# Near scores of a chunked gated linear attention: one product per tile for the diagonal and the levels of 2, 4 and 8

## What is computed

```
b = jnp.cumsum(gi, axis=-2)
o_inter = jnp.einsum('bhtk,bhkv->bhtv', qi * jnp.exp(b), state)
diff = b[:, :, :, None, :] - b[:, :, None, :, :]
decay = jnp.exp(jnp.where(causal, diff, -jnp.inf))
scores = jnp.einsum('bhtk,bhsk,bhtsk->bhts', qi, ki, decay)
o = o_inter + jnp.einsum('bhts,bhsv->bhtv', scores, vi)
```

## Time and profile before

| what | value |
|---|---|
| median of 3 runs | 1216.65 us (1216.47 to 1219.16) |
| the profiled execution | 1214.66 us |
| its span | 1212.5 us |
| TensorE busy | 1183.7 us, 98% of the span |
| VectorE busy | 796.3 us, 66% |
| ScalarE busy | 510.9 us, 42% |
| GpSimd busy | 110.5 us, 9% |

### The profile page before, as it was taken

The page is one execution under the profiler, slowest core; times in us unless marked ns, Lnnn a source line. Parts: engine busy times, 40 slices in busy tenths (PEclk is TensorE's granted clock), DMA queues, the critical chain, the costliest instruction groups (busy, mean ns, idle before and its releaser), DMA issues.

```text
span 1212.5 us, 18972 instructions
## 1 busy us (share of the span) xinstructions
PE 1183.7 (98%) x7577; PEld 1055.5 (87%) x7577; DVE 796.3 (66%) x1071; ACT 510.9 (42%) x646; POOL 110.5 (9%) x166
## 2 busy tenths in 40 slices
PE   6999999999999999999999999999999999999997
PEld 5789999998889987868887788888889999998887
DVE  5788888766786567676563256665878888762232
ACT  6445544561213645455343322233535554552322
POOL 2000000002220123333020001100000000000000
PEclk9999999999999999999999999999999999999999
DMA  9423333337983121212211445633123333322211
GB/s 367 153 73 112 110 108 109 113 99 268 329 293 124 37 69 37 66 39 71 70 62 44 139 157 181 215 108 104 36 73 117 109 109 109 107 96 96 96 61 71
DMA packets 115130, 143.55 MB, mean 118 GB/s; under 512 B 4085, under 2 KB 102785, under 8 KB 115073
## 3 DMA queue, kind: packets, MB, share of 16 engines
q1 hardware_dynamic: 106800, 113.32, 28.2%
q0 software_dynamic: 8064, 29.36, 6.9%
q10 hardware_dynamic: 208, 0.08, 0.0%
HBM read 140.65 MB, written 2.10 MB: 118 GB/s over the span
## 4 chain that ended last, share of the span: by engine, by line
PE 87%; DVE 7%; ACT 4%; issue 1%; POOL 1%; DVEq 0%; ACTq 0%; POOLq 0%
PE PS L794 28%; PE PS L550 16%; PE PS L552 15%; PE PS L551 15%; PE PS L873 4%; PE PS L913 1%; PE PS L595 1%; PE PS L597 1%; PE PS L596 1%; PE PS L708 1%; DVE ACC L1725 1%; ACT WH L1107 1%; PE PS L900 1%; PE PS L883 1%; DVE ACC0b L1736 1%
## 5 line engine op out<-in xcount | busy, mean ns | idle before, releaser
L1623 DVE TENSOR_TENSOR WL<-RAW,WH 128x2048 fp32r<-128x2048 f32 (+2 forms) x55 | 120.6, 2194 | 131.8 <-ACT WH L1107 131.7
L550 PE MATMUL PS<-HH,WH 128*128 128x512 f32 (+2 forms) x488 | 186.4, 382 | 4.3 <-DVE HL L1651 2.9
L1107 ACT ACTIVATE WH<-RAW 128x2048 fp32r<-128x2048 f32 (+2 forms) x55 | 100.6, 1829 | 199.5 <-PE PS L552 193.0
L552 PE MATMUL PS<-HH,WL 128*128 128x512 f32 (+2 forms) x488 | 178.9, 367 | 0.0
L551 PE MATMUL PS<-HL,WH 128*128 128x512 f32 (+2 forms) x488 | 178.8, 366 | 0.0
L794 PE MATMUL PS<-HH,WH 128*128 128x256 f32 x576 | 162.5, 282 | 0.4 <-DVE WL L1910 0.4
L794 PE MATMUL PS<-HL,WH 128*128 128x256 f32 x576 | 162.1, 281 | 0.0
L794 PE MATMUL PS<-HH,WL 128*128 128x256 f32 x576 | 162.1, 281 | 0.0
L550 PE MATMUL PS<-UH,WH 128*128 128x512 f32 (+1 forms) x416 | 148.2, 356 | 0.0
L552 PE MATMUL PS<-UH,WL 128*128 128x512 f32 (+1 forms) x416 | 147.3, 354 | 0.0
L551 PE MATMUL PS<-UL,WH 128*128 128x512 f32 (+1 forms) x416 | 147.2, 354 | 0.0
(11 more groups left out here) (304 smaller groups left out, 2308.4 us busy)
## 6 DMA issues: line engine op xcount, KB each, us to landing
RAW<-in_ffn_w_in_dram SPq DMA_DIRECT2D x42, 1024.0 KB, 5.1
ADAW<-in_w_ada_dram POOLq DMA_DIRECT2D x56, 512.0 KB, 5.4
RAW<-in_w_in_mix_dram SPq DMA_DIRECT2D x22, 1024.0 KB, 5.2
RAW<-in_ffn_w_down_dram SPq DMA_DIRECT2D x16, 1024.0 KB, 5.0
ADA<-in_w_ada_dram SPq DMA_DIRECT2D x16, 512.0 KB, 10.0
RAW<-in_ffn_w_down_dram SPq DMA_DIRECT2D x7, 768.0 KB, 4.3
RAW<-in_w_out_dram SPq DMA_DIRECT2D x3, 1024.0 KB, 5.0
XST<-in_x_dram SPq DMA_DIRECT2D x4, 512.0 KB, 5.1
```

The lines of the kernel that those rows point to most:

```text
L550: mm(ps, whi, ahi, start=start, stop=False)
L552: return mm(ps, wlo, ahi, start=False, stop=stop)
L1107: A(WH[slot(n)][:, 0:size], RAW[slot(n)][:, 0:size], ACT.Copy).then_inc(unit_hi, 1)
L1623: V.tensor_tensor(WL[s][:, 0:size], RAW[s][:, 0:size], WH[s][:, 0:size].bitcast(F32), ALU.subtract)\
```

## The change

The levels of 64, 32, 16 and 8 stay as masks, but only the first three keep a plane of `KP` and of `QP` each. The fourth plane of `KP` now holds every key, all 512 columns, scaled once: its reference is the second token of its quad (four tokens). `QQ` holds for each tile 192 columns: the 128 queries of the tile, scaled against the reference of their own quad, and then 64 queries, the later four tokens of each block of eight, scaled against the reference of the quad before theirs. One product of the fourth plane with these 192 columns gives both the scores within a quad (diagonal and the levels of 2 and 4) and the level of 8. `score_diagonal` is gone. Near0 keeps its eight products; near1 and near2 now each treat two tiles, with one product of 64 and one of 192 columns a tile, and both wait for all near products (`prep` 11 of 15). Near1 uses bank 5 and near2 bank 4; the far product of 256 columns moves from bank 4 to bank 5. A factor within a quad can now exceed one, since the reference token can stand ahead of its key or behind its query; therefore the log decay of a token is held at or above -50 ln 2 (`DECAY_FLOOR`, `LN_FLOOR`).

```diff
-    LN_FLOOR = 2.0 ** -63
+    LN_FLOOR = 2.0 ** -50
+    DECAY_FLOOR = -50 * 0.6931471805599453
...
-        KP = place("KP", [P, 6, T], 69632)
-        QP = place("QP", [P, 6, T // 2], 92160)
+        QP = place("QP", [P, 3, T // 2], 92160)
+        QQ = place("QQ", [P, TT, P + 64], 95232)
...
-        LEVELS = [64, 32, 16, 8, 4, 2]
+        LEVELS = [64, 32, 16, 8]
+        QUAD = 4
+
+        PREP = 15
+
+        def quads(ap):
+
+            return ap.rearrange("p (n b) -> p n b", b=QUAD)
...
                 cc = PREPS[p]["c"]
                 pool.wait_ge(cum, p + 1)
                 if p:
-                    pool.wait_ge(score_done, 6 * before_prep(p) + 3)
-                for l, B in enumerate(LEVELS):
+                    pool.wait_ge(score_done, 5 * before_prep(p) + 3)
+                for l, B in enumerate(LEVELS[0:3]):
                     h = B // 2
                     cb = blocks(cc, B)
                     mid = cb[:, :, h - 1:h].to_broadcast([P, T // B, h])
                     nc.gpsimd.tensor_tensor(QP[:, l, :].rearrange("p (n h) -> p n h", h=h), cb[:, :, h:B], mid,
                                             ALU.subtract).then_inc(diffs, 1)
-                for l, B in enumerate(LEVELS):
+                for l, B in enumerate(LEVELS[0:3]):
                     h = B // 2
                     cb = blocks(cc, B)
                     mid = cb[:, :, h - 1:h].to_broadcast([P, T // B, h])
                     nc.gpsimd.tensor_tensor(blocks(KP[:, l, :], B)[:, :, 0:h], mid, cb[:, :, 0:h],
                                             ALU.subtract).then_inc(diffs, 1)
+                cq = quads(cc)
+                nc.gpsimd.tensor_tensor(quads(KP[:, 3, :]), cq[:, :, 1:2].to_broadcast([P, T // QUAD, QUAD]), cq,
+                                        ALU.subtract).then_inc(diffs, 1)
+                ct = cc.rearrange("p (t n b) -> p t n b", n=P // 8, b=8)
+                nc.gpsimd.tensor_tensor(QQ[:, :, P:P + 64].rearrange("p t (n b) -> p t n b", b=4), ct[:, :, :, 4:8],
+                                        ct[:, :, :, 1:2].to_broadcast([P, TT, P // 8, 4]), ALU.subtract).then_inc(diffs, 1)
...
                 p, r = prep_of(a), rows_of(a)
                 bank = 4 + g % 2
-                pe.wait_ge(prep, 18 * p + 2 + 4 * (g + 1))
+                pe.wait_ge(prep, PREP * p + (6 if g == 0 else 11))
                 if g == 0 and a:
+                    pe.wait_ge(evac_v, a)
+                if g == 1 and a:
                     pe.wait_ge(evac_a, 2 * a)
-                if g == 1 and a:
-                    pe.wait_ge(evac_v, a)
                 if g == 2:
-                    pe.wait_ge(near_done, 6 * a + 2)
+                    pe.wait_ge(near_done, 7 * a + 2)
                 for j in range(2):
-                    l = 2 * g + j
-                    for t in range(TT):
-                        ins = mm(PS[:, bank, 256 * j + 64 * t:256 * j + 64 * t + 64],
-                                 KP[r, l, t * P:(t + 1) * P], QP[r, l, 64 * t:64 * t + 64], start=True, stop=True)
-                ins.then_inc(score_done, 1)
-
-            def score_diagonal(a):
-                p, r = prep_of(a), rows_of(a)
-                q, k = PREPS[p]["q"], PREPS[p]["k"]
-                pe.wait_ge(near_done, 6 * a + 4)
-                for t in range(TT):
+                    if g == 0:
+                        for t in range(TT):
+                            ins = mm(PS[:, bank, 256 * j + 64 * t:256 * j + 64 * t + 64],
+                                     KP[r, j, t * P:(t + 1) * P], QP[r, j, 64 * t:64 * t + 64], start=True, stop=True)
+                        continue
+                    t = 2 * g - 2 + j
                     tok = slice(t * P, (t + 1) * P)
-                    ins = mm(PS[:, 5, tok], k[r, tok], q[r, tok], start=True, stop=True)
+                    mm(PS[:, bank, 64 * j:64 * (j + 1)], KP[r, 2, tok], QP[r, 2, 64 * t:64 * (t + 1)], start=True, stop=True)
+                    ins = mm(PS[:, bank, 128 + 192 * j:128 + 192 * (j + 1)], KP[r, 3, tok], QQ[r, t, :], start=True, stop=True)
                 ins.then_inc(score_done, 1)
 
             def score_far(a):
                 p, r = prep_of(a), rows_of(a)
-                pe.wait_ge(prep, 18 * p + 18)
+                pe.wait_ge(prep, PREP * p + PREP)
                 if a:
                 ins.then_inc(score_done, 1)
-                pe.wait_ge(near_done, 6 * a + 6)
+                pe.wait_ge(near_done, 7 * a + 5)
                 for j in range(2):
-                    ins = mm(PS[:, 4, 256 * j:256 * (j + 1)], W512[r, j * P:(j + 1) * P], W512[r, 256:512],
+                    ins = mm(PS[:, 5, 256 * j:256 * (j + 1)], W512[r, j * P:(j + 1) * P], W512[r, 256:512],
                              start=True, stop=True)
                 ins.then_inc(score_done, 1)
...
                         score_levels(a, 2)
-                        score_diagonal(a)
...
             def near_factors(p):
                 exp_ln_tables()
-                act.wait_ge(diffs, 12 * p + 6)
+                act.wait_ge(diffs, 8 * p + 3)
                 A(QP[:, :, :], QP[:, :, :], ACT.Exp).then_inc(exps, 1)
-                for l, B in enumerate(LEVELS):
-                    act.wait_ge(diffs, 12 * p + 7 + l)
+                for l, B in enumerate(LEVELS[0:3]):
+                    act.wait_ge(diffs, 8 * p + 4 + l)
                     kk = blocks(KP[:, l, :], B)[:, :, 0:B // 2]
                     A(kk, kk, ACT.Exp).then_inc(exps, 1)
+                act.wait_ge(diffs, 8 * p + 7)
+                A(QQ[:, :, 0:P], KP[:, 3, :].rearrange("p (t c) -> p t c", c=P), ACT.Exp, scale=-1.0).then_inc(exps, 1)
+                act.wait_ge(diffs, 8 * p + 8)
+                A(QQ[:, :, P:P + 64], QQ[:, :, P:P + 64], ACT.Exp).then_inc(exps, 1)
+                act.wait_ge(exps, 10 * p + 8)
+                A(KP[:, 3, :], KP[:, 3, :], ACT.Exp).then_inc(exps, 1)
 
             def copy_far(a):
 
-                act.wait_ge(score_done, 6 * a + 5)
+                act.wait_ge(score_done, 5 * a + 4)
                 act.wait_ge(evac_v, a + 1)
                 diag = SC[:, :].rearrange("p (i x) -> p i x", x=5 * P)
                 A(diag[0:64, :, 64:P], PS[0:64, 6, 0:256].rearrange("p (i x) -> p i x", x=64), ACT.Copy)
                 A(SC[:, :].rearrange("p (i x) -> p i x", x=2 * T + 2 * P)[:, :, P:2 * P],
                   PS[:, 6, 256:512].rearrange("p (i x) -> p i x", x=P), ACT.Copy).then_inc(evac_a, 1)
-                act.wait_ge(score_done, 6 * a + 6)
+                act.wait_ge(score_done, 5 * a + 5)
                 A(SC[:, 0:2 * T].rearrange("p (i x) -> p i x", x=T)[:, :, T // 2:T],
-                  PS[:, 4, :].rearrange("p (i x) -> p i x", x=T // 2), ACT.Copy).then_inc(evac_a, 1)
+                  PS[:, 5, :].rearrange("p (i x) -> p i x", x=T // 2), ACT.Copy).then_inc(evac_a, 1)
...
                 dve.wait_ge(exps, 10 * p + 2)
                 V.tensor_tensor(QU[:, :], QU[:, :], q, ALU.mult).then_inc(prep, 1)
                 V.tensor_tensor(KL[:, :], KL[:, :], k, ALU.mult).then_inc(prep, 1)
-                for l, B in enumerate(LEVELS):
+                for l, B in enumerate(LEVELS[0:3]):
                     h = B // 2
                     dve.wait_ge(exps, 10 * p + 4)
                     qp = QP[:, l, :].rearrange("p (n h) -> p n h", h=h)
@@ -2095,8 +2121,16 @@
                     dve.wait_ge(exps, 10 * p + 5 + l)
                     kp = blocks(KP[:, l, :], B)[:, :, 0:h]
                     V.tensor_tensor(kp, kp, blocks(k, B)[:, :, 0:h], ALU.mult).then_inc(prep, 1)
+                dve.wait_ge(exps, 10 * p + 8)
+                V.tensor_tensor(QQ[:, :, 0:P], QQ[:, :, 0:P], q.rearrange("p (t c) -> p t c", c=P), ALU.mult).then_inc(prep, 1)
+                dve.wait_ge(exps, 10 * p + 9)
+                near = QQ[:, :, P:P + 64].rearrange("p t (n b) -> p t n b", b=4)
+                later = q.rearrange("p (t n b) -> p t n b", n=P // 8, b=8)[:, :, :, 4:8]
+                V.tensor_tensor(near, near, later, ALU.mult).then_inc(prep, 1)
+                dve.wait_ge(exps, 10 * p + 10)
+                V.tensor_tensor(KP[:, 3, :], KP[:, 3, :], k, ALU.mult).then_inc(prep, 1)
                 dve.wait_ge(exps, 10 * p + 3)
-                dve.wait_ge(prep, 18 * p + 2)
+                dve.wait_ge(prep, PREP * p + 2)
...
             def copy_near(a):
 
-                for g in range(3):
-                    dve.wait_ge(score_done, 6 * a + g + 1)
-                    for j in range(2):
-                        l = 2 * g + j
-                        h = LEVELS[l] // 2
-                        near = diag.rearrange("p i (n b) -> p i n b", b=2 * h)[:, :, :, h:2 * h]
-                        ps = PS[:, 4 + g % 2, 256 * j:256 * (j + 1)].rearrange("p (i n h) -> p i n h", i=TT, h=h)
-                        m = MASK[:, l, :].rearrange("p (n h) -> p n h", h=h).unsqueeze(1).to_broadcast([P, TT, 64 // h, h])
-                        if l:
```

(29 more changed lines are left out.)

32 lines of the change are left out of this document (21 added, 11 removed).

## The result

The changed kernel takes 1188.28 us (median of 4 runs, 1187.77 to 1188.77) against 1217.37 us of the kernel before beside it (4 runs, 1216.47 to 1219.16): ratio 0.9759, 95% interval 0.9742 to 0.9776, so 29.1 us faster. The forecast was 1193 us in a range from 1188.5 to 1203.5: the kernel became faster, by more than the range allows. The profiled execution took 1188.77 us, its span is 1186.9.

What follows compares the result with a forecast made beforehand. TensorE, busy 98% of the span, was taken as the bound. Passes 18.7, waits 3.5 and clock 1.2 sum to 23.4 us off 1214.66, giving 1191.3; plus 2.0 for the median, 1193 us (range 1188.5 to 1203.5).

Steps and rivals of the forecast that it cites:

- The passes: TensorE's near1 and near2: 16 products a head instead of 28, saving 2.34 us a head, 18.7 in eight heads.
- rival 1: TensorE's 192-column pass costs only 0.111 us, saving 3.4 us more, time 1189.6; chance 0.08.
- the dear pass: Upper bound for TensorE's 192-column pass, 0.217 us as at 256 columns: passes save 15.4 us.
- Waits: TensorE's mixer waits: 3.2 of 3.6 us for VectorE's key products and 0.3 for the decay table go, 3.5 in all.
- Near1 would not starve: Near1 now waits for all near products; a slack of 1.0 us after near0 hides this.
- rival 4: Last key product late, TensorE stands still at near1 six times; 5.5 us each gives 1226 us; chance 0.03.
- The chains follow: Work leading into near0 starts at TensorE products, so it moves earlier with TensorE and the waits do not grow.
- rival 2: Chains into near0 hang on something fixed in time; heads 1 to 3 give back 7.0 us: 1203; chance 0.14.
- No term for the position: Mask building and floors were said to cost nothing; the sum had no term for buffers moving.
- The median carried over: The shown runs' median is 2.0 us above the profiled execution; this was added to 1191.3, giving 1193.
- The clock term itself: The one slow-clock stretch, near 642 us, six projection passes at 0.43 instead of 0.23, vanishes: 1.2 us gained.
- rival 3: The clock falls more often: a 1.2 us slow stretch in each of eight heads, old one staying, 1204; chance 0.10.

Runs made afterwards that it cites:

- the padded kernel before: The kernel before with 128 bytes of unused memory per partition, shifting every buffer behind it as the change does: 1215.17 us, ratio 0.9973.
- the repeat: The kernel before, unchanged, run and profiled once more: 1218.33 us, ratio 0.9998.
- +192: The changed kernel with 64 unused bytes per partition behind the masks: 1184.60 us, ratio 0.9730 to the kernel before.
- +224: The changed kernel with 96 unused bytes per partition behind the masks: 1200.18 us, ratio 0.9847 to the kernel before.

## Why the prediction was right or wrong

- *What bounds the kernel*, and that a microsecond off TensorE's queue comes off the total: right. 22.9 us in the mixer for 23.4.
- *The passes*: right in size, 18.2 us for 18.7, with a pass of 192 columns at 0.164 (halfway between 0.111 and 0.217; width alone gives 0.163). In the first branch a tile's four passes took 0.55 us as reckoned, so rival 1 (0.44 with passes of 0.111) and the dear pass (0.66 with 0.217) fell. But all prices were taken from head 0. In the second branch's heads the old and the new stages are both dearer (2.03 and 1.39 us for 1.78 and 1.10), and that this leaves the difference nearly as it was is luck. Nor do 128 columns cost no more than 64: 2.76 - 1.78 is 0.98 us for eight passes, 0.12 each.
- *Waits*: 3.5 us forecast; from 3.9 to 1.0 it is 2.9, and 2.5 with all rows. The reason given, GpSimd's shorter run, is shown from both sides (longer again: 4.8; lighter in the kernel before: 1.9). The remainder was put at 0.4 and is 1.0, and it was VectorE's own queue.
- *Near1 would not starve* (rival 4): right, slack 1.1 for 1.0. *The chains follow* (rival 2's opposite): right, by the kernel with only TensorE's products changed.
- *No term for the position*: the first step that failed, and the larger one. The forecast says that the mask building and the floors "cost nothing: the masks are made in the first microseconds and used far later". Making them shows no cost (the changed kernel reaches the mixer at 437.94, the padded kernel before at 439.52), but their size moves all later buffers by 128 bytes. The kernel before with this shift alone is 3.3 us faster, and behind the mixer, where the forecast had no change at all, it takes 529.65 us for 533.75. Between the two profiled executions the work outside the mixer differs by 3.0 us (4.1 less behind it, 1.4 more ahead, 0.3 around the span).
- *The median carried over*: the second step that failed. "The median of the runs shown is 2.0 above it, and I carry this over" assumes that what lifts the kernel before's median over its profiled execution is there in the changed kernel too. It wasn't: the changed kernel's median is 0.5 below its profiled execution. The likely content of these 2.0 us is half-clock stretches. The profiled execution had one in the mixer and a mean clock of 0.996; the repeat has four and 0.993; and of the 72 later runs of the kernel before, the 16 with a mean clock of 0.996 or more average 1215.7 us, the 22 with 0.990 or less 1219.4. The three runs behind that median have no clock on record, so this stays likely, not shown. This step gives 2.5 of the miss (2.0 and 0.5).
- *The clock term itself*, 1.2 us for one stretch: right for the execution that it was read from (1.4), and rival 3 is out. For the kernels it was too small, since the kernel before has more such stretches in most executions: about 3.5 us.

The 3.0 and the 2.5, less 0.5 too much in the mixer, are the miss of 5.0 (1193.25 to 1188.28). Either step alone would have left the result in the range, which had no room for both.

At equal position, passes (18.2), waits (5.1 in the padded kernel before to 2.1, so 3.0) and clock (3.5) come to 24.7, and 25.5 was measured, give or take 2.5.

## What to carry to other kernels

A float32 pass took 0.111 us at 64 columns, 0.12 at 128, about 0.164 at 192 and 0.217 at 256, so join products that share weights, and look for waits that shrink with the preparation. Take the price of a product from each of its forms: with 64 rows the stages here were dearer. Read the clock of several executions before sizing a clock term, and don't carry over the gap between one execution and the median without knowing what it is made of. When a change alters any buffer's size, run the old kernel with the same shift, or its effect and the position's are not told apart; and compare a stage that the change doesn't touch, since a difference there belongs to something else.

## What the runs showed that was not expected

- A shift of buffers by 32 bytes changes the pace of TensorE's passes at full clock and equal traffic: 256 to 265 passes of 512 columns in 60 us, 1166 to 1191 of 256 columns in 140 us. Between two positions of one program, the changed kernel at +192 and +224, lie 15.6 us (14.3 by the ratios to the kernel before beside each).
- The clock fell to half within a stretch in which TensorE was busy in 20.00 of 20 us, where runs of small float32 products with 64 rows had been doubled; doubled runs with 128 rows left it full in the same execution.
- A small float32 product between two 512-column passes costs the same 0.23 us as in a row of its like.
